# An encoder trunk on one core: the norms' squares summed by TensorE, three chunks at the start of a channel mixer, and the down loads in another order

## The chip, the core and the metric

The kernel runs on one core of a Trainium2 chip. The metric is device time in microseconds. The core has a tensor engine (PE; its weight loads are shown apart as PEld), a vector engine (DVE), a scalar engine (ACT), GpSimd (POOL) and a queue that issues DMAs (SP). Each runs its own list of instructions in order; semaphores tie them together.

## The reference

Two batches (prompt and sample) of 512 tokens with 1024 features pass a trunk of two layers with shared weights, in float32. Layer 0 mixes tokens by windowed means, layer 1 by attention; each is followed by a SwiGLU channel mixer.

```python
def trunk(x, ...):
    for i in range(DEPTH):                       # 2
        h = rms_norm(x, norm_mix[i])
        if i % N_MIXERS == 0: x = x + pool_mixer(h, ...)
        else:                 x = x + attention_mixer(h, ...)
        h = rms_norm(x, norm_ffn[i])
        x = x + swiglu_ffn(h, ...)               # (silu(h Wg) * (h Wu)) Wd, hidden size 2816
def rms_norm(x, g):
    return x * rsqrt(mean(x * x, axis=-1) + EPS) * g
```

## The kernel before

x lies in the on-chip memory with features on the 128 partitions: 8 tiles of features (c) by 2 batches (b) of 512 tokens. Every float32 product is made of three products of split operands: each operand is cast to a rounded high part (ACT) and a low part, the rest (DVE, `..._lo`), and PE multiplies high by high, high by low and low by high.

**Channel mixer.** The two batches and the two halves of each weight matrix form a 2x2 block product, which is computed with seven block products instead of eight (`gate_up(layer, i, k)`, k = 1 to 7). The hidden size is taken in 22 chunks i of 128. One product is 12 matmuls. The moving operands B11, B21 (batch 0), T1, T2, B22, T3, T4 (sums with batch 1) are made once per layer: `b0_full`, `b1_full` scale x by the norm, `t1_full` to `t4_full` subtract (T3 and T4 on POOL, in float32), and `..._hi`, `..._lo` split. The weights of a chunk come as two units (gate and up) into three buffers `raw` (`load_gu`); `block_sums` makes their sums S1 to S4, and `w_split` splits seven tiles into `ring`. `snap_p1`, `snap_p5`, `snap_u2` copy partial sums out of PSUM, `add_c11`, `add_c12`, `add_c22` add to them, `silu_0`, `silu_1`, `hidden_0`, `hidden_1` and `pair_sums` make the hidden values and their sums, which SP stores to device memory (`store_act1`, `store_even`, `store_odd`). Chunks use two sets of three PSUM banks in turn. In the steady state the order of PE is 1, 5, 6, 3, 7, 2, 4. For chunks 0 to 2, where T1 to T4 aren't there yet, the order is written out by hand.

**Down products.** 42 blocks of up to 24 matmuls (`down_block(layer, k)`): for each, ACT and DVE split a piece of weights and a piece of stored hidden values (`block_hi`, `block_lo`). `down_sum(layer, n)` makes weight sums on DVE between the blocks. SP loads hidden pieces (`load_act`, which from the fourth on waits for `block_lo` three blocks before) and weight pieces (`load_wd`; two pieces jj share a semaphore, and a reader waits for both).

**Norm.** For each norm k (1: channel mixer of layer 0; 2: attention; 3: channel mixer of layer 1) ACT squares the tiles of x (`square`), in the order `SEQ[k]`; POOL adds them one by one into `stat[b]` (`add_squares`); PE multiplies that by a matrix of ones, which leaves the sum over all features in every partition (`mean_square`); ACT takes the root of the 128x512 tile (`root`) and DVE its reciprocal (`inverse`). The mixers' work around it is written in order for every engine: in layer 0, PE's `pool(b, c)` (windowed means), `turn_x` (x turned to features on partitions) and `mix(b, g)` (projection), and DVE's `add_mixed`, which adds to x. In attention, `project` makes queries and keys, and `gain`, `head_square` their norm.

## Time and profile before

| | |
|---|---|
| median of 3 runs | 1824.36 us (1822.15 to 1827.1) |
| profiled execution, own time | 1823.22 us |
| its span | 1821.4 us |
| mean granted clock of PE | 0.976 of full |
| PE busy | 1717.3 us (94%), 7741 instructions |
| DVE busy | 1205.1 us (66%) |
| ACT busy | 760.7 us (42%) |
| POOL busy | 202.0 us (11%) |

Times in the rows are microseconds from the span's start. Layer 0's token mixer runs until about 75, its gate/up products until 523, its down blocks until 741, attention until about 1110 to 1144, then layer 1's channel mixer. PEclk and the column of the same meaning in a table of windows give the clock that the chip granted to PE, as a share of 2.4 GHz; 0.5 is 1.2 GHz. In a timeline row the figures are start, time from the first start to the last end, engine, line, operation, operands, count, and in brackets how long the engine had been idle and what it waited for. A busy time of PE overlaps the next instruction's, so lengths are read from start to start.

### The profile page before, as it was taken

The numbers are of one execution on the slowest core, as the hardware profiler recorded it, in microseconds if no ns is written. First come the engines' busy times: TensorE is split into PE (matmuls) and PEld (weight loads), VectorE is DVE, ScalarE is ACT, GpSimd is POOL, SyncE is SP. The second block draws the span as 40 slices with busy tenths as digits, with TensorE's granted clock in tenths as the row PEclk, the third lists the DMA queues.
The fourth block names the chain that finished last, engine by engine and source line by source line (L and its number), as shares of the span: only waits on it lengthen the run. The fifth ranks groups of instructions, "written<-read, shape, count | busy, mean of one in ns | idle before, by whom it ended". The sixth has DMA issues, their size and how long they took to land. (4 is left out here: it accounts for less than half of the span.)

```text
span 1821.4 us, 20998 instructions
## 1 busy us (share of the span) xinstructions
PE 1717.3 (94%) x7741; PEld 1409.0 (77%) x7741; DVE 1205.1 (66%) x1620; ACT 760.7 (42%) x1149; POOL 202.0 (11%) x155
## 2 busy tenths in 40 slices
PE   6779999999999999899998999799999999989998
PEld 6657888888877888778776787578888888878887
DVE  5786656666547756756878877876566665557744
ACT  6543333333333335434576554343333333333332
POOL 1430000000000003322124212500000000000000
PEclk9889999999999999999999999899999999999999
DMA  4003423224275332143112112023233232473333
GB/s 170 24 12 121 129 90 113 93 93 133 76 270 197 101 94 90 58 133 103 42 54 63 35 47 81 24 93 116 87 109 117 93 116 87 156 289 116 95 98 120
DMA packets 185786, 188.40 MB, mean 103 GB/s; under 512 B 8355, under 2 KB 138453, under 8 KB 185685
## 3 DMA queue, kind: packets, MB, share of 16 engines
q1 hardware_dynamic: 112884, 150.36, 25.5%
q10 hardware_dynamic: 72800, 36.70, 6.9%
q8 instruction: 62, 1.02, 0.2%
q14 instruction: 40, 0.32, 0.1%
HBM read 137.23 MB, written 44.56 MB: 100 GB/s over the span
## 5 line engine op out<-in xcount | busy, mean ns | idle before, releaser
L664 PE MATMUL bank<-h_T,ring 128*128 128x512 f32 x2112 | 508.9, 393 | 20.0 <-DVE h_T L1512 11.2
L664 PEld LDWEIGHTS bank<-h_T,ring 128*128 128x128 f32 x2112 | 399.8, 190 | 108.6 <-issue 10.8
L689 PE MATMUL bank<-a,w 128*128 128x512 f32 x1848 | 426.1, 393 | 10.9 <-DVE a L1638 10.9
L689 PEld LDWEIGHTS bank<-a,w 128*128 128x128 f32 x1848 | 349.8, 190 | 85.8 <-issue 12.9
L664 PE MATMUL bank<-h_B,ring 128*128 128x512 f32 x1584 | 388.9, 395 | 9.9 <-ACT tmp L1037 4.3
L664 PEld LDWEIGHTS bank<-h_B,ring 128*128 128x128 f32 x1584 | 300.6, 190 | 78.4 <-ACT tmp L1037 5.2
L1565 DVE TENSOR_TENSOR ring<-raw,ring 128x512 fp32r<-128x512 f32 (+1 forms) x178 | 147.7, 831 | 48.3 <-ACT ring L1016 48.1
L1016 ACT CAST ring<-raw 128x512 fp32r<-128x512 f32 (+1 forms) x178 | 128.5, 722 | 69.7 <-PE bank L664 53.7
L1090 ACT CAST w<-wd_A 128x1024 fp32r<-128x1024 f32 x72 | 70.6, 981 | 199.8 <-PE bank L689 199.8
L1634 DVE TENSOR_TENSOR w<-wd_A,w 128x1024 fp32r<-128x1024 f32 x72 | 82.6, 1147 | 97.3 <-ACT w L1090 97.2
L2112 POOL TENSOR_TENSOR tmp<-tmp,tmp 128x512 f32<-128x512 f32 x42 | 62.5, 1488 | 749.8 <-ACT tmp L938 747.5
L546 PE MATMUL bank<-half_hi,aw 128*128 128x512 f32 x320 | 111.9, 408 | 4.6 <-DVE aw L1459 3.9
L1577 DVE TENSOR_TENSOR tmp<-bank,tmp 128x512 f32<-128x512 f32 x44 | 30.4, 691 | 124.9 <-PE bank L664 124.6
L1638 DVE TENSOR_TENSOR a<-raw,a 128x1024 fp32r<-128x1024 f32 x84 | 97.0, 1154 | 6.5 <-ACT a L1092 6.5
L1092 ACT CAST a<-raw 128x1024 fp32r<-128x1024 f32 x84 | 82.0, 977 | 13.1 <-DMA raw<-act_d 13.1
L546 PE MATMUL bank<-o_hi,aw 128*128 128x512 f32 x256 | 85.6, 397 | 1.5 <-DVE x L1979 1.5
L1016 ACT CAST ring<-s_tmp 128x1024 fp32r<-128x1024 f32 (+1 forms) x46 | 46.7, 1015 | 91.2 <-PE bank L664 85.2
L1343 ACT ACTIVATE prob<-bank,nmax,q_inv 128x512 f32<-128x512 f32 x64 | 49.9, 780 | 70.7 <-DVE nmax L1956 70.7
L546 PEld LDWEIGHTS bank<-half_hi,aw 128*128 128x128 f32 x320 | 61.4, 192 | 19.5 <-issue 3.7
L1053 ACT ACTIVATE tmp<-tmp 128x512 f32<-128x512 f32 x44 | 27.8, 631 | 103.0 <-DVE tmp L1583 103.0
L1565 DVE TENSOR_TENSOR ring<-s_tmp,ring 128x1024 fp32r<-128x1024 f32 (+1 forms) x46 | 54.1, 1177 | 20.7 <-ACT ring L1016 20.7
L1459 DVE TENSOR_TENSOR aw<-raw,aw 128x1024 fp32r<-128x1024 f32 x40 | 54.7, 1369 | 16.6 <-ACT aw L925 16.1
(168 smaller groups left out, 2097.9 us busy)
## 6 DMA issues: line engine op xcount, KB each, us to landing
act_d<-tmp SPq DMA_DIRECT2D x154, 256.0 KB, 3.0
raw<-in_ffn_w_gate_up ACTq DMA_DIRECT2D x70, 512.0 KB, 3.9
raw<-act_d SPq DMA_DIRECT2D x70, 512.0 KB, 3.5
wd_A<-in_ffn_w_down SPq DMA_DIRECT2D x40, 512.0 KB, 6.7
raw<-in_attn_w_qkv SPq DMA_DIRECT2D x24, 512.0 KB, 3.9
raw<-in_ffn_w_gate_up SPq DMA_DIRECT2D x18, 512.0 KB, 4.2
raw<-in_attn_w_o SPq DMA_DIRECT2D x16, 512.0 KB, 4.2
tmp<-tmp SPq DMA_DIRECT2D x80, 64.0 KB, 2.0
```

The lines of the kernel that those rows point to most:

```text
L546: ins = pe.matmul(out, w, m, start=first and i == 0, stop=last and i == n - 1)
L664: ins = pe.matmul(out[:, :], w, m, start=k in (1, 2, 5) and j == 0 and t == 0, stop=k in (2, 3, 4) and j == 3 and t == 2, skip_group_check ...
L689: ins = pe.matmul(banks[m][:, :], w, h, start=q in (0, 1, 3) and first and t == 0, stop=q in (1, 5, 6) and jj == NBLK - 1 and t == 2, skip ...
L1016: nc.scalar.copy(dst, src).then_inc(f_hi, 1)
L1090: nc.scalar.copy(w2[:, k % 3, 0:n, 0, :], src).then_inc(w2_hi, 1)
L1092: nc.scalar.copy(a2[:, (k + 1) % 3, 0:n, 0, :], raw2[:, act_slot(layer, k), 0:n, :]).then_inc(a2_hi, 1)
L1343: nc.scalar.activation(prob[:, i, :], b_score[s % 2][:, :], ACT.Exp, bias=nmax[:, s % 8:s % 8 + 1], scale=q_inv[:, s:s + 1], accum_out=rsu ...
L1459: nc.vector.tensor_tensor(aw[:, slot(i), 1, :], raw[:, i % RAW, :], aw[:, slot(i), 0, :].bitcast(F32), ALU.subtract).then_inc(w_lo, 1)
L1565: nc.vector.tensor_tensor(lo, src, hi.bitcast(F32), ALU.subtract).then_inc(f_lo, 1)
L1634: nc.vector.tensor_tensor(w2[:, k % 3, 0:n, 1, :], src, w2[:, k % 3, 0:n, 0, :].bitcast(F32), ALU.subtract).then_inc(w2_lo, 1)
L1638: nc.vector.tensor_tensor(a2[:, s, 0:n, 1, :], raw2[:, act_slot(layer, k), 0:n, :], a2[:, s, 0:n, 0, :].bitcast(F32), ALU.subtract).then_i ...
L2112: nc.gpsimd.tensor_tensor(out=stat[b][:, :], in0=stat[b][:, :], in1=sqr[i % 2][:, :], op=ALU.add).then_inc(n_acc, 1)
```

## The change

`square` puts some tiles, the set `DIRECT[k]`, into a ring of free tiles. For those PE itself sums over features: `columns` multiplies a square tile (stationary, four times 128x128) by a column of ones and adds into 4 columns of PSUM. For norm 1 all 16 tiles are `DIRECT`, for norm 2 the last four, for norm 3 the last one. What POOL still adds goes through the same `columns`. The result has tokens on partitions, 128x4. ACT takes the root of these 4 columns, DVE their reciprocal and multiplies the unit matrix by it (`diag`), PE multiplies ones by the diagonal (`wide`, 128x512), and ACT copies the result to `stat[b]` (`keep_wide`), or, for `b1_full` of the first four tiles, DVE reads it in PSUM.

A layer's gate/up products begin with chunks 0, 1 and 2, chunk 2 with a third set of banks; its products 1 and 2 move to the start. The tiles of `act_tiles` are laid out anew: three for each chunk; T4 goes to the tile of B11 (after its store), and `silu_0` writes the tile that `silu_1` had. SP stores T1 and B21 ahead of `load_gu(3, 1)`; two A12 pieces are loaded ahead of the last stores, and A21 and A22 come in pairs; `down_sum(n)` follows block n + 4 instead of n + 3. The split of S3 and A12 for chunk 0 comes earlier on ACT and DVE.

The diff, cut to its core:

```diff
+        sq_ring = {1: [tmp[4], tmp[5], tmp[2], tmp[1]], 2: [tmp[4], tmp[5], tmp[0]], 3: [tmp[2]]}
+        diag = {1: tmp[3], 2: tmp[1], 3: tmp[0]}
-        g_bank = [bank[0:3], bank[3:6]]
+        g_bank = [bank[0:3], bank[3:6], [bank[6], bank[7], bank[2]]]
+        DIRECT = {1: SEQ[1], 2: SEQ[2][12:], 3: SEQ[3][15:]}
...
             if i % 2:
-                return act_y
+                return tmp[4], tmp[5], tmp[6]
-            return act_x if j % 2 == 0 else [act_x[3], act_x[1], act_x[2], act_x[0]]
+            return (tmp[0], tmp[1], tmp[2]) if j % 2 == 0 else (tmp[3], tmp[7], tmp[2])
...
+            def columns(src, out, first):
+                for i in range(NT):
+                    ins = pe.matmul(out[:, i:i + 1], src[:, i * P:(i + 1) * P], ones[:, 0:1],
+                                    start=first and i == 0, stop=True, skip_group_check=True)
+            def sum_square(k, r, out):
+                pe.wait_ge(n_sq, 16 * (k - 1) + r + 1)
+                ins = columns(sq_tile(k, r), out, k == 1 and c == 0)
+                ins.then_inc(n_add, 1)
             def mean_square(k, b, out):
-                pe.matmul(out[:, :], ones[:, :], stat[b][:, :], start=True, stop=True).then_inc(n_ms, 1)
+                return columns(stat[b], out, True)
+            def wide(k, b, out):
+                pe.wait_ge(n_diag, 2 * (k - 1) + b + 1)
+                pe.matmul(out[:, :], ones[:, :], diag[k][:, :], start=True, stop=True).then_inc(n_wide, 1)
...
                 for b in range(N_BLOCK):
                     if layer == 0 and b == N_BLOCK - NBLK + 2:
-                        mean_square(2, 0, bank[1])
+                        mean_square(2, 0, bank[1]).then_inc(n_ms, 1)
+                    elif layer == 0 and b == N_BLOCK - NBLK + 4:
+                        wide(2, 0, bank[1])
...
             def inverse(k, b):
                 dve.wait_ge(n_sqrt, 2 * (k - 1) + b + 1)
-                nc.vector.reciprocal(stat[b][:, :], stat[b][:, :]).then_inc(n_rstd, 1)
+                nc.vector.reciprocal(cols, cols).then_inc(n_rstd, 1)
+                nc.vector.tensor_tensor(diag[k][:, :]..., ident[:, :]..., cols..., ALU.mult).then_inc(n_diag, 1)
...
             def silu_0(layer, i):
-                if j > 0 and i % 2 == 0:
-                    act.wait_ge(stored["T3"], 16 * j)
-                elif j > 0:
-                    act.wait_ge(stored["T4"], 16 * j)
+                act.wait_ge(act1, n + 1)
...
-                    if 3 <= k < 27:
-                        down_sum(layer, k - 3)
+                    if 4 <= k < 28:
+                        down_sum(layer, k - 4)
...
-            for r in range(8):
-                add_squares(1, r)
             block_sums_13(0, 0)
             block_sums_24(0, 0)
-            for r in range(8, 16):
-                add_squares(1, r)
```

PE at the start of layer 0's channel mixer, before (L559 is `mean_square`; h_B_80 is B11, h_B_81 is B21, h_T_86 is T1, h_T_82 is T2; a row of L664 or L725 is one product):

```order
L664 MATMUL bank<-h_B_80,ring 128x512 x12
L559 MATMUL bank<-tmp_77,ones 128x512
L664 MATMUL bank<-h_B_81,ring 128x512 x12
L664 MATMUL bank<-h_B_80,ring 128x512 x12
L664 MATMUL bank<-h_T_86,ring 128x512 x12
L664 MATMUL bank<-h_B_81,ring 128x512 x12
L664 MATMUL bank<-h_T_86,ring 128x512 x12
L664 MATMUL bank<-h_T_82,ring 128x512 x12
```

And after, from the same product on (L577 is `columns`, L598 is `wide`):

```order
L725 MATMUL bank<-h_B_80,ring 128x512 x12
L577 MATMUL bank<-ones,tmp_72 128x1 x4
L577 MATMUL bank<-ones,tmp_71 128x1 x4
L725 MATMUL bank<-h_B_81,ring 128x512 x12
L598 MATMUL bank<-tmp_73,ones 128x512
L725 MATMUL bank<-h_B_80,ring 128x512 x12
L725 MATMUL bank<-h_B_81,ring 128x512 x12
L725 MATMUL bank<-h_B_80,ring 128x512 x12
L725 MATMUL bank<-h_T_86,ring 128x512 x12
L725 MATMUL bank<-h_B_81,ring 128x512 x12
L725 MATMUL bank<-h_T_86,ring 128x512 x12
L725 MATMUL bank<-h_T_82,ring 128x512 x12
```

Two products with B operands, (2, 1) and (2, 2), now stand ahead of and between the first ones with T1, and the two last tiles of squares ahead of the second product.

PE at the end of layer 0's down blocks, before (L689 is the down products; 84 are the last four blocks, of 24, 24, 24 and 12):

```order
L664 MATMUL bank<-h_T_84,ring 128x512 x12
L689 MATMUL bank<-a_107,w_106 128x512 x840
L559 MATMUL bank<-tmp_76,ones 128x512
L689 MATMUL bank<-a_107,w_106 128x512 x84
L546 MATMUL bank<-half_hi_50,aw 128x512
```

And after (L750 is the down products):

```order
L725 MATMUL bank<-h_T_84,ring 128x512 x12
L750 MATMUL bank<-a_107,w_106 128x512 x840
L577 MATMUL bank<-ones,tmp_76 128x1 x4
L750 MATMUL bank<-a_107,w_106 128x512 x48
L598 MATMUL bank<-tmp_71,ones 128x512
L750 MATMUL bank<-a_107,w_106 128x512 x36
L564 MATMUL bank<-half_hi_50,aw 128x512
```

The sum is taken at the same place; the product that gives every partition the norm comes two blocks, 48 matmuls, later.

SP behind the last stores of layer 0, before (raw_108 takes the hidden pieces of the down blocks; wd_A_101 is A12, wd_A_102 is A21, wd_A_103 is A22):

```order
L407 DMA raw_108<-act_d 128x1024
L388 DMA wd_A_101<-in_ffn_w_down 128x2x512 x2
L407 DMA raw_108<-act_d 128x1024
L388 DMA wd_A_102<-in_ffn_w_down 128x2x512
L388 DMA wd_A_103<-in_ffn_w_down 128x2x512
L407 DMA raw_108<-act_d 128x512
L388 DMA wd_A_101<-in_ffn_w_down 128x2x512 x2
L407 DMA raw_108<-act_d 128x1024
L388 DMA wd_A_102<-in_ffn_w_down 128x2x512
```

And after:

```order
L424 DMA raw_108<-act_d 128x1024
L405 DMA wd_A_102<-in_ffn_w_down 128x2x512 x2
L424 DMA raw_108<-act_d 128x1024
L405 DMA wd_A_103<-in_ffn_w_down 128x2x512 x2
L424 DMA raw_108<-act_d 128x512
L405 DMA wd_A_101<-in_ffn_w_down 128x2x512 x2
L424 DMA raw_108<-act_d 128x1024
```

The second piece of A21 stood behind the fourth hidden piece of this list and now stands behind the first.

## Rows read from the trace of the kernel before

**Rows 1.** Windows, engine PE: stretch, length, busy (instructions), clock, DMA share, GB/s.
```profile
45.00:140.00 95.00, 73.07 (x295) 0.84 0.08 24
140.00:330.00 190.00, 187.86 (x829) 1.00 0.34 106
```

**Rows 2.** Timeline of PE, start of layer 0's channel mixer.
```profile
41.19 3.22 PE L595 MATMUL bank<-band,xrms 128*128 128x136 f32 x24
47.58 2.07 PE L559 MATMUL bank<-tmp,ones 128*128 128x512 f32 x2 [3.18 <-POOL tmp L2112]
...
56.50 0.47 PE L546 MATMUL bank<-half_hi,pw_hi 128*128 128x512 f32 x1 [0.48 <-ACT x L1111]
...
83.00 2.08 PE L559 MATMUL bank<-tmp,ones 128*128 128x512 f32 x2 [8.53 <-POOL tmp L2112]
...
131.30 5.60 PE L664 MATMUL bank<-h_T,ring 128*128 128x512 f32 x24
136.74 2.88 PE L664 MATMUL bank<-h_B,ring 128*128 128x512 f32 x12
...
149.91 0.50 PE L664 MATMUL bank<-h_B,ring 128*128 128x512 f32 x1 [2.14 <-ACT tmp L1037]
```

**Rows 3.** Timeline of DVE, the same stretch.
```profile
50.41 3.35 DVE L1465 RECIPROCAL tmp<-tmp 128x512 f32<-128x512 f32 x1 [2.59 <-ACT tmp L943]
...
57.33 1.41 DVE L1488 SCALAR_TENSOR_TENSOR f_t<-x,vec,tmp 128x512 f32<-128x512 f32 x2
...
89.66 1.50 DVE L1501 SCALAR_TENSOR_TENSOR f_t<-x,vec,tmp 128x512 f32<-128x512 f32 x1
...
102.32 0.74 DVE L1501 SCALAR_TENSOR_TENSOR f_t<-x,vec,tmp 128x512 f32<-128x512 f32 x1
...
107.83 0.69 DVE L1565 TENSOR_TENSOR ring<-raw,ring 128x512 fp32r<-128x512 f32 x1 [1.09 <-ACT ring L1016]
...
116.39 5.74 DVE L1531 TENSOR_TENSOR h_B<-f_t,h_B 128x512 fp32r<-128x512 f32 x4
```

**Rows 4.** Timeline of ACT: the last moves of x.
```profile
53.10 3.11 ACT L1111 ACTIVATE x<-bank,vec 128x512 f32<-128x512 f32 x5 [0.17 <-PE bank L579]
```

**Rows 5.** Timeline of PE in attention: the sum of one head's squares, and what follows.
```profile
787.33 1.05 PE L781 MATMUL bank<-ones,tmp 128*128 128x1 f32 x8 [1.81 <-ACT tmp L1276]
788.25 0.48 PE L546 MATMUL bank<-half_hi,aw 128*128 128x512 f32 x1
```

**Rows 6.** Timelines of PE and DVE, start of attention.
```profile
721.71 19.65 PE L689 MATMUL bank<-a,w 128*128 128x512 f32 x84
742.97 0.50 PE L546 MATMUL bank<-half_hi,aw 128*128 128x512 f32 x1 [1.61 <-DVE aw L1459]
...
728.79 1.41 DVE L1474 SCALAR_TENSOR_TENSOR tmp<-x,vec,tmp 128x512 f32<-128x512 f32 x2
```

**Rows 7.** Timelines of PE and DVE, start of layer 1's channel mixer.
```profile
1116.79 0.47 PE L546 MATMUL bank<-o_hi,aw 128*128 128x512 f32 x1 [1.54 <-DVE x L1979]
...
1144.08 2.88 PE L664 MATMUL bank<-h_B,ring 128*128 128x512 f32 x12
...
1216.48 4.61 PE L664 MATMUL bank<-h_B,ring 128*128 128x512 f32 x12 [2.20 <-ACT tmp L1037]
...
1156.92 0.80 DVE L1501 SCALAR_TENSOR_TENSOR f_t<-x,vec,tmp 128x512 f32<-128x512 f32 x1
```

**Rows 8.** Timelines of PE and DVE and a window of PE, start of the down blocks.
```profile
549.96 25.40 PE L689 MATMUL bank<-a,w 128*128 128x512 f32 x100 [4.62 <-DVE a L1638]
...
1618.90 31.47 PE L689 MATMUL bank<-a,w 128*128 128x512 f32 x128 [4.82 <-DVE a L1638]
...
546.31 1.23 DVE L1652 TENSOR_TENSOR wd_A<-wd_A,wd_A 128x1024 f32<-128x1024 f32 x1 [10.93 <-DMA wd_A<-in_ffn_w_down]
...
525.00:528.00 3.00, 3.00 (x15) 1.00 0.37 137
```

**Rows 9.** Timelines of DVE and PE, chunk 21 of layer 0: hidden_1, and the last product.
```profile
518.85 0.69 DVE L1589 TENSOR_TENSOR tmp<-tmp,tmp 128x512 f32<-128x512 f32 x1 [0.70 <-ACT tmp L1053]
...
519.98 2.88 PE L664 MATMUL bank<-h_T,ring 128*128 128x512 f32 x12
```

416 lines of the change are left out of this document (264 added, 152 removed).

## The prediction

> **What bounds the kernel now.** I read the table of windows first, then PE's timeline for its idle times, then DVE's and ACT's in the same stretches. The windows [rows 1] show two kinds of stretch: in 140:330 PE is busy 187.86 of 190 us at full granted clock, and there only PE's own work counts; in 45:140 it is busy 73.07 of 95 at a mean clock of 0.84. PE's waits are in few places, and the change touches nearly all of them: the start of each layer's channel mixer (waits of 3.18 and 8.53 us for POOL's sums of squares [rows 2], then a stretch in which DVE has no gap [rows 3]), one wait of 2.14 us [rows 2], the fifth block of the down products, and the start of attention. So the sum is made at five places. Measures used throughout: a gate/up product of 12 matmuls takes 2.72 us at full clock (24 of them from 131.30 to 136.74, [rows 2]), a down block of 24 takes 5.44; a DVE operation on 128x512 takes 0.6 to 0.7 us from start to start.
>
> **Price of the new small sums.** Each square that PE sums is four matmuls of one moving column, eight instructions. The trace has the same pattern for the query heads: it starts at 787.33 and the next matmul at 788.25, so 0.92 us [rows 5]. There are 25 of them: 16 for layer 0's second norm, 4 + 2 in the attention norm, 1 + 2 in the last; 23 us of PE. What they replace are six products of 512 columns, but each norm half now has one such product (the wide one, about 1.0 us at full clock, as before) as well.
> The Trainium skill, TensorE: Matmul & The Clock Gate, section Back-to-back issue gap, gives a floor of about 25 ns from start to start for so few columns; eight would be 0.2 us. Its section on LDWEIGHTS gives 107 ns for each load of 128 columns, 0.86 us for eight. The measured 0.92 us goes with the second; by the first, the 25 sums would cost 5 us instead of 23.
>
> **Down blocks, both layers.** DVE's subtraction for block 4 stands behind down_sum(0), which sat 10.93 us on a weight load (A21's second piece), and PE then waited 4.62 us [rows 8]. The load was issued behind act load 6, which itself waited for block_lo(3). After: both A21 pieces are issued right behind act load 3 and down_sum(0) comes after block_lo(4), so neither is in the way. What could be late next is act load 3, now behind two A12 pieces: block 3 is needed 16.3 us after the first down product, and those pieces go out at 521 to 522, where the DMA engines have room (share 0.37 from 525 to 528, [rows 8]). I take the whole wait as gone. The following 100 matmuls took 25.40 us where 22.9 is full rate, since the granted clock had fallen in the wait: 2.5 more. Layer 1: 4.82 of wait, and 31.47 for 128 instead of 29.2 [rows 8]. Together 14.2 us gained; ends: 7 (half of the waits come back as late transfers) and 14.2.
>
> **Layer 0, start.** PE finishes pool(1, 2) at 44.4 [rows 2]. Four sums end at 48.1, four turns of x (0.12 us per transpose, 1.9) at 50.0, four sums at 53.7, four turns at 55.6, the wide product at 56.5. ACT is behind it: squares 4 to 7 wait for free tiles until 48.7, three casts, then eight moves of 0.61 [rows 4] and a root of 0.3 until 56.7. So mix(1, 0) starts at 57.4 (56.50 before), and b0_full at 58.7 (57.33 before, [rows 3]): nothing is won here, although 3.18 us of wait and the reciprocal of 3.35 us [rows 3] go. From there until gate_up(0, 2) ends PE has four mixes (10.9), four pools (4.1), two products (5.4), eight sums (7.4) and the wide product (0.9), 28.7 us, plus some 1.9 in which it waits for DVE's additions to x: b1_full(0) at 88.0, 89.66 before [rows 3]. The 8.53 us of wait is thus mostly eaten by sums and by the later start. b1_full(4) came 12.7 us later [rows 3] and now has one DVE operation more before it (101.3), then the 1.09 us wait of a ring split on ACT goes [rows 3], since snap_p5 now stands ahead of three casts: B22 is finished at 119.9 rather than 122.1. PE ends product (0, 3) about 1 us later, 2.1 earlier than before; and it has done two products more by then, (2, 1) and (2, 2), worth 5.44. Given back later: with those two no longer as filling, (1, 4) and (2, 4) each wait for add_c22 (0.85 each), (2, 5) waits for S1 of chunk 2, behind c22, hidden_1 and four block sums (1.8), and (2, 7) for snap_u2 behind a split that needs the late unit (3, 1) (0.8): 4.3. The 2.14 us wait of (2, 3) at 149.91 [rows 2] is for tile T1's store, which SP issued behind that same unit and now ahead of it: gained. Sum: 2.1 + 5.4 - 4.3 + 2.1 = 5.4 gained. Bounds: -1 (ACT's order behind the sums costs 4 more, the whole of it DVE's) and 10 (no ping-pong, no gaps).
>
> **Layer 1, start.** Its batch-0 norm: the sum is taken after projection 8 instead of 9, so root and inverse are done when the wide product comes; b0_full starts 2.6 us earlier, and the wait of 1.54 us at 1116.79 goes [rows 7] for 0.9 of extra sum. gate_up(0, 1) then starts at 1143.5 (1144.08, [rows 7]); with it 2.72, two sums 1.84, gate_up(0, 2) 2.72 and the wide product 0.9, b1_full is at 1152.0 rather than 1156.92 [rows 7]: here POOL's last two additions and the reciprocal stood on the path, and little PE work takes their place. From there as in layer 0: 4.9 - 0.6 + 1.1 + 5.4 - 4.3 + 2.2, and 1.7 because the products after 1216.48 ran at half clock (4.61 for 12 instead of 2.88, [rows 7]): 10.4. Bounds 5 and 14.
>
> **Attention, start.** This part costs. The sum of squares is ready before block 38, as before, but the reciprocal now returns as a diagonal, and the wide product that spreads it stands in PE's order before block 40, two blocks of 5.44 later. PE: 721.2 + 0.9 + 10.9 + 0.9 = 733.9, ACT's copy 734.5; norm_full(0, 0) starts at 734.6, not at 728.79 [rows 6]. The whole chain to the first weight split hangs on it, so the first projection comes at 748.8, not 742.97 [rows 6]; PE is through with the down blocks at 742.2 and stands still 6.6 us instead of 1.6, long enough for its clock to fall (it fell in the waits of 4.6). In the first projection PE then has five sums, 4.6 us, in place of a 1.98 us wait and a product. The second half's norm_full starts about 8.5 later. Behind it PE waited 0.56 + 1.65 + 2.27 us for DVE, which takes up what PE is later than DVE; I come out at +6.5. Bounds +2 (all of the later half absorbed) and +10.
>
> **Sum.** -14.2 - 5.4 - 10.4 + 6.5 = -23.5 on the profiled execution's 1823.22 us, which is 1.1 under the median of the runs: 1799.7, taken as **1800**. Its own range, 1792 to 1808.
>
> **Rivals.**
> (1) The small sums and ACT's order eat the starts: layer 0 gives nothing, layer 1 gives 7, attention costs 9. For it: in 57:75 PE was already without a gap, and DVE too [rows 2, 3]. Then 14 + 0 + 7 - 9 = 12: **1811**.
> (2) The down wait is only shifted, since the transfers are near their limit there: half of 14.2 stays, 7: **1807**. Against it: the A12 pieces go out when the queue has room.
> (3) The sums hide and attention's late wide product is absorbed: 14.2 + 10 + 12 - 4 = 32: **1791**. By the page's floor for one column (0.2 us each) this is the case; the row of 0.92 us speaks against it, as does PE's own order of the wide product.
> (4) Slower: silu_0 now writes the tile that hidden_1 reads and so waits for it, in each of 44 chunks. hidden_1 starts at 518.85 and the product that silu_0 waits for anyway ends at 522.9 [rows 9]; the slack is 3.3 us. If something at the steady rate pushes hidden_1 past it, each further microsecond costs 1 us in some 40 chunks, and from 4 us of delay on the kernel is slower: 1800 + 40 = **1840**. Against it: the page has DVE busy for only 66% of the span, and its waits in a chunk are for PE.
> (5) The change does not act: the starts and attention cancel and the down wait is replaced by another: **1822**.
>
> **Chances.** Forecast 0.50, (1) 0.20, (2) 0.08, (3) 0.13, (4) 0.03, (5) 0.06. Faster by over 0.3% (under 1818, about what a measurement of this kernel can tell) is all but (4), (5) and a sliver of (1): 0.89. Same: 0.07. Slower: 0.04. The range 1788 to 1814 takes in (1), (2) and (3) but for their tails.
>
> **What would show it.** In the changed kernel's trace: no PE idle between down blocks 3 and 4; sums of about 0.92 us; b1_full near 88 in layer 0 and 5 us earlier against the layer's start in layer 1; idle of 0.8 to 1.8 us before products (1, 4), (2, 5) and (2, 4), and none before (2, 3); the longest PE wait of the kernel (over 6 us) before the first projection, with half clock behind it. The prediction is wrong if norm_full(0, 0) doesn't come after the wide product by two blocks, if PE waits at block 4 as before, or if steady chunks take more than 19.04 us.

## The result, and the profile after

| | before | changed |
|---|---|---|
| median of the runs | 1823.66 us (6 runs, 1822.15 to 1827.1) | 1815.18 us (6 runs, 1812.64 to 1820.76) |
| profiled execution | 1823.22 us, span 1821.4 | 1813.04 us, span 1811.0 |

The changed kernel takes 0.995 of the time before, 95% interval 0.9932 to 0.9968: faster by 8.5 us, where 24 were forecast. The time lies just outside the predicted range.

The windows answer to [rows 1]. In 45:140 PE is now busy 84.62 us, not 73.07, at a clock of 0.93 and not 0.84, and still layer 0's first down product comes only 1.4 us earlier: the waits were filled with the work of the new norm.

```profile
45.00:140.00 95.00, 84.62 (x426) 0.93 0.07 20
140.00:330.00 190.00, 186.78 (x822) 1.00 0.35 110
```

PE's timeline at layer 0's start in the changed kernel, for [rows 2]. A pair such as (1, 4) is chunk 1, product 4. The first five rows are the first half of the norm, with no gap between them; a wait of 2.52 us for a split comes before (2, 1); then waits where the forecast had them, before (1, 4), (2, 5), (2, 7) and (2, 4), and none before (2, 3).

```profile
43.77 3.63 PE L577 MATMUL bank<-ones,tmp 128*128 128x1 f32 x32
47.26 1.95 PE L619 MATMUL bank<-ident,xin 128*128 128x128 f32 x16
49.04 3.66 PE L577 MATMUL bank<-ones,tmp 128*128 128x1 f32 x32
52.56 3.57 PE L619 MATMUL bank<-ident,xin 128*128 128x128 f32 x16
55.97 1.02 PE L598 MATMUL bank<-tmp,ones 128*128 128x512 f32 x2
...
97.84 3.02 PE L725 MATMUL bank<-h_B,ring 128*128 128x512 f32 x12 [2.52 <-DVE ring L1683]
...
138.96 3.06 PE L725 MATMUL bank<-h_T,ring 128*128 128x512 f32 x12 [0.78 <-DVE tmp L1701]
143.57 5.69 PE L725 MATMUL bank<-h_T,ring 128*128 128x512 f32 x24 [1.56 <-DVE ring L1683]
152.86 3.02 PE L725 MATMUL bank<-h_T,ring 128*128 128x512 f32 x12 [0.88 <-ACT tmp L1141]
156.66 3.04 PE L725 MATMUL bank<-h_T,ring 128*128 128x512 f32 x12 [0.78 <-DVE tmp L1701]
```

Four sums of squares take 3.49 us (43.77 to 47.26), 0.87 each, where [rows 5] gave 0.92. The 16 transposes at 47.26 take 1.78, the same 16 at 52.56 take 3.41: the clock has fallen to half between, though PE never stood still. DVE's timeline of the same stretch, for [rows 3]: `b1_full(0)` at 91.12 behind a wait of 1.72 us for a split, where 88.0 was forecast, and B22's low parts at 117.25, where before they began at 116.39.

```profile
59.21 1.41 DVE L1600 SCALAR_TENSOR_TENSOR f_t<-x,vec,tmp 128x512 f32<-128x512 f32 x2
...
89.67 1.53 DVE L1683 TENSOR_TENSOR ring<-raw,ring 128x512 fp32r<-128x512 f32 x1 [1.72 <-ACT ring L1110]
91.12 0.73 DVE L1618 SCALAR_TENSOR_TENSOR f_t<-x,vec,bank 128x512 f32<-128x512 f32 x1
...
102.67 0.74 DVE L1618 SCALAR_TENSOR_TENSOR f_t<-x,vec,tmp 128x512 f32<-128x512 f32 x1
...
117.25 5.14 DVE L1648 TENSOR_TENSOR h_B<-f_t,h_B 128x512 fp32r<-128x512 f32 x4
```

Attention's start, PE, DVE and a window of PE (length, busy, clock, DMA share, GB/s), for [rows 6]. The diagonal is ready at 714.68; DVE finishes two splits and then has nothing to do for 8.91 us, because the wide product stands in PE's order behind two down blocks. PE pays 6.64 us before the first projection and works at a clock of 0.55 behind it; another 3.85 before projection 2.

```profile
713.99 0.69 DVE L1575 TENSOR_TENSOR tmp<-ident,n_inv 128x512 f32<-128x512 f32 x1
...
725.99 1.42 DVE L1586 SCALAR_TENSOR_TENSOR tmp<-x,vec,tmp 128x512 f32<-128x512 f32 x2 [8.91 <-ACT tmp L1038]
```
```profile
724.31 1.02 PE L598 MATMUL bank<-tmp,ones 128*128 128x512 f32 x2
...
740.17 0.80 PE L564 MATMUL bank<-half_hi,aw 128*128 128x512 f32 x1 [6.64 <-DVE aw L1566]
...
777.87 0.77 PE L564 MATMUL bank<-half_hi,aw 128*128 128x512 f32 x1 [3.85 <-DVE aw L1566]
```
```profile
525.00:528.00 3.00, 3.00 (x15) 1.00 1.05 406
740.00:746.00 6.00, 5.83 (x15) 0.55 0.47 130
```

Down blocks, for [rows 8]: both layers run from their first products without the waits of 4.62 and 4.82 us, though the DMA share in 525:528 is now 1.05 and not 0.37. (Each row ends where the next other instruction or the end of the view stands.)

```profile
521.88 178.44 PE L750 MATMUL bank<-a,w 128*128 128x512 f32 x786 [0.42 <-DVE a L1757]
...
1588.90 185.23 PE L750 MATMUL bank<-a,w 128*128 128x512 f32 x816 [1.17 <-DVE a L1757]
```

Layer 1's start, PE and DVE, for [rows 7]. From its first product (1148.46; its row starts there) to `b1_full` it is now 8.97 us, 12.84 before.

```profile
1148.46 1.75 PE L725 MATMUL bank<-h_B,ring 128*128 128x512 f32 x7
...
1165.25 4.59 PE L725 MATMUL bank<-h_B,ring 128*128 128x512 f32 x12 [2.99 <-DVE ring L1683]
```
```profile
1157.43 0.73 DVE L1618 SCALAR_TENSOR_TENSOR f_t<-x,vec,bank 128x512 f32<-128x512 f32 x1
```

To compare kernels I cut each profile at seven points of PE's timeline: the first gate/up product of layer 0 (GU0), its first down product (DN0), the end of its down products, the start of projection 2 (P2), the first product of layer 1 (GU1), its first down product (DN1), the end of the span. Stretches in us:

| profile of | to GU0 | GU0 to DN0 | down 0 | to P2 | P2 to GU1 | GU1 to DN1 | to end |
|---|---|---|---|---|---|---|---|
| before | 71.6 | 451.7 | 218.1 | 35.5 | 367.2 | 448.0 | 229.4 |
| changed | 81.4 | 440.5 | 211.7 | 44.3 | 370.6 | 440.4 | 222.1 |
| e1_down_only | 69.5 | 453.6 | 210.7 | 35.5 | 371.2 | 448.8 | 222.1 |
| e11_down_t1 | 69.4 | 450.6 | 210.7 | 35.4 | 369.9 | 446.7 | 222.1 |
| e13_last_norm_only | 69.0 | 451.7 | 210.7 | 35.5 | 370.0 | 443.0 | 222.1 |
| e2_wide_early | 88.3 | 442.1 | 211.6 | 36.5 | 370.7 | 442.0 | 222.0 |
| e3_wides_early | 80.3 | 440.4 | 211.6 | 37.2 | 368.4 | 441.6 | 222.0 |
| e4_norm2_old | 86.8 | 439.5 | 210.7 | 35.5 | 367.1 | 443.9 | 223.7 |
| e5_wide_sums | 78.8 | 443.3 | 211.6 | 44.0 | 368.0 | 440.9 | 222.1 |
| e8_two_chunks | 81.5 | 439.5 | 211.6 | 43.3 | 369.2 | 443.4 | 222.1 |
| e6_norm1_pool | 70.5 | 454.2 | 211.6 | 47.8 | 366.9 | 441.3 | 222.1 |
| e12_norm3_old | 81.3 | 439.5 | 211.6 | 46.4 | 370.7 | 448.7 | 223.7 |

Each row is one execution, and the rows come from several chips. The column P2 to GU1, which the change hardly touches, differs by 4 us among kernels alike there: less than that in one profile proves nothing by itself. Part of it is the clock. By the records of the granted clock, the five profiles with less than 16 us at half clock in that stretch have 366.9 to 368.4 us (one of them, e9, is not in the table), the two with 22 us (changed, e2) have 370.6 and 370.7; those with 17 us lie anywhere from 367.2 to 371.2.

### The profile page after: what moved, and what is told of

It reads as the page before. It is cut to its first block, busy times and chain, and to the rows that moved or that the text cites. A ratio compares the mean times of both kernels' runs of the same rounds, so it can differ in the third digit from the quotient of the medians.

```text
span 1811.0 us, 21412 instructions
## 1 busy us (share of the span) xinstructions
PE 1732.8 (96%) x7941; PEld 1428.2 (79%) x7941; DVE 1187.2 (66%) x1628; ACT 761.9 (42%) x1157; POOL 175.2 (10%) x136
## 3 DMA queue, kind: packets, MB, share of 16 engines
q8 instruction: 64, 1.05, 0.2%
## 4 chain that ended last, share of the span: by engine, by line
PE 41%; DVE 4%; issue 2%; ACT 2%; DMA 1%; SPq 0%; POOLq 0%; POOL 0%; DVEq 0%; ACTq 0%
PE bank L725 21%; PE bank L750 12%; PE bank L564 7%; DVE raw_max L2090 1%; ACT pt_hi L1482 1%; PE bank L920 1%; DVE pt_lo L2144 0%; ACT aw L1005 0%; DMA raw<-act_d 0%; DVE nmax L2096 0%; PE bank L772 0%; DVE aw L1566 0%; DVE ring L1683 0%; DVE f_t L1618 0%; DMA raw<-in_ffn_w_gate_up 0%
## 5 line engine op out<-in xcount | busy, mean ns | idle before, releaser
L725 PE MATMUL bank<-h_T,ring 128*128 128x512 f32 x2112 | 502.6, 390 | 16.6 <-DVE ring L1683 6.8
L725 PEld LDWEIGHTS bank<-h_T,ring 128*128 128x128 f32 x2112 | 395.4, 188 | 104.2 <-issue 8.4
L750 PE MATMUL bank<-a,w 128*128 128x512 f32 x1848 | 421.2, 390 | 1.6 <-DVE a L1757 1.6
L750 PEld LDWEIGHTS bank<-a,w 128*128 128x128 f32 x1848 | 346.5, 188 | 74.5 <-issue 2.9
L725 PE MATMUL bank<-h_B,ring 128*128 128x512 f32 x1584 | 388.4, 395 | 7.0 <-DVE ring L1683 5.5
L725 PEld LDWEIGHTS bank<-h_B,ring 128*128 128x128 f32 x1584 | 299.9, 190 | 74.5 <-DVE ring L1683 6.4
L1181 ACT CAST w<-wd_A 128x1024 fp32r<-128x1024 f32 x72 | 70.5, 979 | 177.7 <-PE bank L750 177.7
L564 PE MATMUL bank<-half_hi,aw 128*128 128x512 f32 x320 | 117.7, 427 | 11.8 <-DVE aw L1566 10.5
L1757 DVE TENSOR_TENSOR a<-raw,a 128x1024 fp32r<-128x1024 f32 x84 | 97.2, 1157 | 13.3 <-ACT a L1183 13.3
L2252 POOL TENSOR_TENSOR tmp<-tmp,tmp 128x512 f32<-128x512 f32 x23 | 35.0, 1520 | 656.3 <-ACT tmp L1025 655.6
L1110 ACT CAST ring<-s_tmp 128x1024 fp32r<-128x1024 f32 (+1 forms) x46 | 46.7, 1015 | 82.6 <-PE bank L725 80.3
L564 PE MATMUL bank<-half_lo,aw 128*128 128x512 f32 x160 | 66.3, 414 | 0.0
```

What stands on the lines that cost most here:

```text
L564: ins = pe.matmul(out, w, m, start=first and i == 0, stop=last and i == n - 1)
L725: ins = pe.matmul(out[:, :], w, m, start=k in (1, 2, 5) and j == 0 and t == 0, stop=k in (2, 3, 4) and j == 3 and t == 2, skip_group_check ...
L750: ins = pe.matmul(banks[m][:, :], w, h, start=q in (0, 1, 3) and first and t == 0, stop=q in (1, 5, 6) and jj == NBLK - 1 and t == 2, skip ...
L1110: nc.scalar.copy(dst, src).then_inc(f_hi, 1)
L1181: nc.scalar.copy(w2[:, k % 3, 0:n, 0, :], src).then_inc(w2_hi, 1)
L1757: nc.vector.tensor_tensor(a2[:, s, 0:n, 1, :], raw2[:, act_slot(layer, k), 0:n, :], a2[:, s, 0:n, 0, :].bitcast(F32), ALU.subtract).then_i ...
```

## The experiments

Ratios are to the kernel before, of runs on the same chip; the changed kernel stands at 0.995 (0.9932 to 0.9968). A difference between two ratios whose intervals overlap is called open.

**e1_down_only.** Before, with the changed order of A21, A12 and A22 loads, two A12 pieces ahead, and:

```diff
-                    if 3 <= k < 27:
-                        down_sum(layer, k - 3)
+                    if 4 <= k < 28:
+                        down_sum(layer, k - 4)
```

> The kernel before, with only the third part of the change: the order of the weight loads for the down products, and down_sum one block later. Theory A (the parts add up, and the down part is worth what the forecast said): no wait at down block 4 in either layer, 14.2 us off the kernel before, 1809.5. Theory B (part of that gain in the changed kernel came from its shifted starts): 7 us or less, 1816 or more.

Measured: 1812.6 us, ratio 0.9935 (0.9918 to 0.9952), 11.3 us under before; in the profile 7.4 and 7.3 us in the two down stretches. Theory A for the mechanism and, by the profile, the size; the median lies between the two theories, nearer to A, and the profile lost 4.0 us of the gain between P2 and GU1. This part alone does all that the whole change does: what the rest of it is worth in sum can't be told from nothing.

**e2_wide_early.** The changed kernel with one line:

```diff
-                    elif layer == 0 and b == N_BLOCK - NBLK + 4:
+                    elif layer == 0 and b == N_BLOCK - NBLK + 3:
                         wide(2, 0, bank[1])
```

> The changed kernel with the attention norm's first wide product one block of 24 earlier (before down block 39 and not 40). Theory A (DVE's idle 8.9 us before the first norm_full are PE's own order, and they come out as PE's 6.64 us before the first projection): norm_full starts near 720.6 instead of 725.99, the wait is 1.6, and since the clock no longer falls there another 1 to 2 us come back: 6 to 7 us under the changed kernel, 1808 to 1809. Theory B (the second half of the norm sets the end of this stretch, since its squares come from the last rows of the down products, which do not move): PE's waits move to the projections behind it, and 0 to 2 us are left, 1813 to 1815.

Measured: 1805.92 us, ratio 0.9899 (0.988 to 0.9919). Theory A: PE waits 1.21 us before the first projection, and from the last down product to projection 2 it is 36.5 us and not 44.3. The median is the thing to read here: the profiled execution is the slowest of the six (1815.15 us), and its fall of the clock before GU0 is the longest of all profiles. The same place in the next run's profile, DVE and then PE: norm_full at 719.36, 13.0 us before the end of the down products, where it was 7.6 before it in the changed kernel: earlier by the one block of 5.44 us.

```profile
719.36 1.42 DVE L1586 SCALAR_TENSOR_TENSOR tmp<-x,vec,tmp 128x512 f32<-128x512 f32 x2 [3.49 <-ACT tmp L1038]
```
```profile
717.69 1.02 PE L598 MATMUL bank<-tmp,ones 128*128 128x512 f32 x2
...
733.56 0.50 PE L564 MATMUL bank<-half_hi,aw 128*128 128x512 f32 x1 [1.21 <-DVE aw L1566]
```

**e3_wides_early.** That, and:

```diff
             project(0, b_gate[0], 0, 3)
+            wide(2, 1, b_up[1])
             project(1, b_gate[1], 0, 0)
             project(1, b_gate[1], 0, 1)
-            wide(2, 1, b_up[1])
```

> As the run before, and the second half's wide product right behind projection 0, two quarters of a projection earlier (near 755.6 and not 757.88). Theory A (each wide product's place in PE's order delays DVE): the wait of 3.85 us before projection 2 shrinks by the 2.3 us, 8 to 9 us in all under the changed kernel, 1806 to 1807. Theory B (POOL's split of the second half, 2.5 us for two parts, sets the pace there): no change against the run before.

Measured: 1803.64 us, ratio 0.9888 (0.9868 to 0.9908). PE's wait before projection 2 shrank from 3.85 to 2.95 only, and the stretch did not get shorter (37.2): theory B for the second product, and the difference of the medians to e2_wide_early is open.

**e4_norm2_old.** The changed kernel with the attention norm as before.

```diff
-        DIRECT = {1: SEQ[1], 2: SEQ[2][12:], 3: SEQ[3][15:]}
+        DIRECT = {1: SEQ[1], 2: [], 3: SEQ[3][15:]}
...
-            mean_square(2, 1, b_up[1])
-            for r in range(12, 16):
-                sum_square(2, r, b_up[1])
+            mean_square(2, 1, b_down[3]).then_inc(n_ms, 1)
```

> The changed kernel with the attention norm in the form of before: POOL sums all squares, a sum over 512 columns, root and reciprocal of the whole tile, no wide product, orders of the three engines as before. Theory A (the new form costs 13 us by the attention's leads, 743 to 1022, and not the 6.5 of the forecast): 12 to 13 us under the changed kernel, 1802 to 1803. Theory B (part of the 13 us is the normal loss when PE arrives earlier at a stretch set by DVE and DMA): 6 to 7 us under, 1808 to 1809.

Measured: 1806.01 us, ratio 0.9899 (0.9875 to 0.9924), 9.2 us under the changed kernel by the medians, and 35.5 us to projection 2 instead of 44.3: 8.9. It lies between the two theories, 2.4 above the forecast's 6.5. The stretch behind P2 runs from 366.9 to 371.2 over the table's twelve profiles, with the old norm and the new in no order, so the 3.4 us that the changed kernel's profile lost there are not the norm's.

**e5_wide_sums.** The changed kernel; each square of layer 0's second norm is summed by one product that accumulates over the eight of its half:

```diff
-                ins = columns(sq_tile(k, r), out, k == 1 and c == 0)
-                ins.then_inc(n_add, 1)
+                if k == 1:
+                    pe.matmul(out[:, :], ones[:, :], sq_tile(k, r)[:, :], start=c == 0, stop=c == KC - 1,
+                              skip_group_check=True).then_inc(n_add, 1)
```

> The changed kernel; in layer 0's second norm each square is summed by one product of 512 columns against the tile of ones, eight of them accumulating in one bank, in place of four products of one column; root and reciprocal then go over the whole 128x512 tile, and the two wide products that spread the inverse go. Theory A (the price of the small sums and what they do to the granted clock made layer 0's start no gain): a float32 product of 512 columns takes 0.46 us from start to start (757.88 to 758.33 in the changed kernel's trace), a small sum 0.92, so 16 times 0.46 or 7.4 us of PE less, the clock stays at 1.0 between 44 and 57 us, and after two reciprocals of 3.35 us some 4 to 8 us are left: 1807 to 1811, with the first down product before 519 us. Theory B (DVE sets the pace of that start whatever PE does): the reciprocals stand on the path again and nothing is won, 1814 to 1818.

Measured: 1812.43 us, ratio 0.9929 (0.9913 to 0.9946): open against the changed kernel and between the two theories, with the runs within 5.2 us of each other and the first down product at 522.0, not before 519. One number of the expectation was wrong: four such sums take 3.43 us, 0.86 each, as much as the small ones, not 0.46 (the row that I had taken it from overlaps with its neighbour). So what this run tells is the clock. PE's timeline, then windows with clock in 44:60 for this kernel and for e2_wide_early, which has the small sums:

```profile
43.62 3.60 PE L591 MATMUL bank<-tmp,ones 128*128 128x512 f32 x8
47.05 1.91 PE L626 MATMUL bank<-ident,xin 128*128 128x128 f32 x16
48.80 3.60 PE L591 MATMUL bank<-tmp,ones 128*128 128x512 f32 x8
52.24 1.91 PE L626 MATMUL bank<-ident,xin 128*128 128x128 f32 x16
```
```profile
44.00:60.00 16.00, 15.41 (x81) 1.00 0.01 2
```
```profile
44.00:60.00 16.00, 16.00 (x88) 0.57 0.01 2
```

**e14_first_half_wide.** The same for the first eight squares only, the second eight as changed:

```diff
+                if k == 1 and b == 0:
+                    pe.matmul(out[:, :], ones[:, :], sq_tile(k, r)[:, :], start=c == 0, stop=c == KC - 1,
+                              skip_group_check=True).then_inc(n_add, 1)
+                    return
```

> The changed kernel with the sums of only the first half of layer 0's second norm (the eight between 44 and 57 us) as accumulating products of 512 columns; the second half's eight stay sums of one column. Theory A (the fall of the granted clock in 44 to 60 us follows those eight small sums and the transposes among them): the clock there stays at 1.0 in the profile, the runs keep within 6 us of each other and the kernel comes at 1810 to 1812. Theory B (all sixteen, or PE's busy stretch without a gap, bring it down): the clock falls as in the changed kernel, 1813 to 1816.

Measured: 1814.24 us, ratio 0.9947 (0.9929 to 0.9964); the clock in 44:60 is 1.00 again, the runs lie within 6.5 us. Theory A for the clock and nearly for the spread, theory B for the time.

```profile
44.00:60.00 16.00, 15.41 (x80) 1.00 0.01 2
```

The fall did not go away, it moved: behind the first two of the small sums that are left (at 64.02 us) the clock is at half from 66.4 to 69.8 us. The same 16 windowed-mean matmuls in this profile and in that of e5_wide_sums, which has no fall there, with the same wait of 0.59 us before the sums:

```profile
65.83 3.52 PE L639 MATMUL bank<-band,xrms 128*128 128x136 f32 x16
```
```profile
65.73 2.07 PE L642 MATMUL bank<-band,xrms 128*128 128x136 f32 x16
```

All profiles together: the seven kernels with the small sums there have a clock of 0.57 (once), 0.61 (twice) or 0.89 (four times) in 44:60, and GU0 between 80.3 and 88.3 us; the four with sums over 512 columns have 1.00 in all and GU0 between 78.3 and 81.3. The five where POOL sums have 1.00 three times, 0.79 and 0.89, each with a wait of PE of 3.2 us just before. The runs of one kernel spread by 8 to 14 us in the first group (5 to 12 runs each), 5 to 7 in the second (4 to 6 runs), 2 to 9 in the third (4 to 17 runs): that the small sums make the times spread is likely, not shown.

**e6_norm1_pool.** The changed kernel with layer 0's second norm on POOL, as before:

```diff
-        DIRECT = {1: SEQ[1], 2: SEQ[2][12:], 3: SEQ[3][15:]}
+        DIRECT = {1: [], 2: SEQ[2][12:], 3: SEQ[3][15:]}
...
-            for c in range(4):
-                sum_square(1, c, bank[3])
-            turn_x(1, range(4))
...
+            mean_square(1, 0, bank[3]).then_inc(n_ms, 1)
+            turn_x(1, range(KC))
```

> The changed kernel with layer 0's second norm as before: POOL adds up the squares, one product per half, root and reciprocal of the whole tile; the start with three chunks stays. Theory A (the small sums cost more than POOL's sums made PE wait): the first down product comes at 518 to 520 us in every run, where four profiles of kernels with the small sums had 520.7, 521.9, 526.3 and 530.4, so 3 to 6 us under the changed kernel, 1809 to 1812. Theory B (the forecast: waits of 3.18 and 8.53 us come back and cost what the sums cost): 1815 to 1820.

Measured: 1818.23 us, ratio 0.9958 (0.9943 to 0.9974). DN0 at 524.6, where it is 520.0 in e11_down_t1, which has the same sums and two chunks: PE waits 10.86 us before the sum of the second half and 5.19 before a product of the new order, and over the whole way to DN0 it is idle 4.6 us longer than in e11. Theory B: three chunks begun do not help while the norm comes late.

**e7_split_later.** The changed kernel; in both layers on DVE:

```diff
-                w_split(layer, 1, G_A12)
                 b1_full(layer, 0)
                 t1_full(layer, 0)
+                w_split(layer, 1, G_A12)
```

> The changed kernel, and on DVE in both layers the split of A12 of chunk 1 behind b1_full(0) and its sum, not ahead of them. Theory A (DVE sets PE's pace from b1_full(0) to tile T4, and b1_full(0) waits for this split, 1.72 us of wait and 1.5 of work): b1_full(0) starts at about 89.7 instead of 91.12, and 1 to 2 us are won in each layer, 1811 to 1814. Theory B (the split's wait is only moved: product (1, 2) or DVE waits for it behind b1_full): no change, 1815.

Measured: 1821.67 us (12 runs, 1811.44 to 1824.13), ratio 0.9968 (0.9953 to 0.9984). Theory B: its profile and that of e4_norm2_old have the same clock in 44:60 (0.61), the same GU0 (86.8) and the same stretch to DN0, 439.5, with the split ahead or behind. Its median is above the changed kernel's since nine of the twelve runs lie at 1820 or more and three at 1811 to 1815; the profile is one of the nine, with the long fall of the clock. The mean granted clock of each run goes with this: 0.984 in the three, 0.978 to 0.982 in the nine. That it is the fall in 44:60 which parts the two groups is likely, not shown: no execution of the three has a profile.

**e8_two_chunks.** The changed kernel with the orders of before for the gate/up products on all three engines; on PE:

```diff
                 gate_up(layer, 1, 1)
-                gate_up(layer, 1, 2)
-                gate_up(layer, 2, 1)
                 gate_up(layer, 0, 5)
-                gate_up(layer, 2, 2)
+                gate_up(layer, 1, 2)
                 gate_up(layer, 1, 5)
...
                 gate_up(layer, 1, 7)
+                gate_up(layer, 2, 1)
                 gate_up(layer, 1, 4)
```

> The changed kernel with each layer's gate/up products begun by two chunks in the orders of before on PE, ACT and DVE; norms, tiles, loads and the down part stay as changed. Theory A (the forecast's own balance: 5.4 us from two products done early, 4.3 given back): 1 us per layer slower, 1817. Theory B (layer 1's gain of 6 to 8 us from its first product to its first down product, 440.4 to 443.9 in five profiles against 448.0 and 448.8 in two of the old start, is the three chunks'): layer 1's stretch takes 448 again, and layer 0 loses as much: 1823 to 1829. Theory C (it is the last norm's, whose inverse no longer takes 3.35 us of DVE): layer 1's stretch stays at 441 to 444, 1815.

Measured: 1813.7 us, ratio 0.995 (0.9934 to 0.9966). Theory C, and for layer 0 as well: GU0 to DN0 takes 439.5 us with two chunks, 440.5 with three. In layer 0 the waits of 0.78 to 1.56 us before (1, 4) to (2, 4) are gone again (0.29 is left of them), and nothing is lost for it: up to 125 us PE waits 9.9 us here and 8.3 in the changed kernel, so the two products done early took 1.6 us out of the waits and not 5.44. B22's low parts begin at 115.70, where the changed kernel has 117.25. In layer 1 the stretch is 3.0 us longer, but PE's idle time in it is the same (11.2 and 11.3 us), and PE is at half clock for 17.1 us instead of 6.8. The third chunk is worth nothing that these runs can tell.

```profile
115.70 5.75 DVE L1646 TENSOR_TENSOR h_B<-f_t,h_B 128x512 fp32r<-128x512 f32 x4
```

**e9_sums_wides** has the edits of e5 and e3, shown above, and nothing else; **e10_sums_norm2** those of e5 and e4.

> The changed kernel with the 512-column sums of the run e5_wide_sums and both wide products of the attention norm early, as in e3_wides_early. If the two causes are separate, their gains add: 3.8 us and 11.5 us under the changed kernel, 1799 to 1802, with a spread of the runs near the 5 us of e5_wide_sums and not the 12 of e4_norm2_old. If both had their gain from the same thing (the granted clock over the whole run), the larger stands alone, 1804.

> The changed kernel with the 512-column sums in layer 0's second norm, and the attention norm as before (as in e4_norm2_old). From the first kernel's profile to projection 2 the old norm takes 35.4 us from the last down product, the two early wide products 37.2: 0 to 2 us faster than e9_sums_wides by that, 1798 to 1801; slower than it, 1803, if POOL's four sums of the second half (1.95 us of wait for PE) weigh more.

Measured: 1802.99 us, ratio 0.9885 (0.9872 to 0.9898), and 1803.76 us, 0.9889 (0.9877 to 0.9902), within 5.5 and 4.6 us. Not the sum that was expected: to e3_wides_early (0.9888) the wide sums added nothing that can be measured; its runs spread by 8.5 us, but four or five runs are few to compare spreads by.

**e11_down_t1.** e1 and one line's place on SP:

```diff
                 store_act1(layer, 0)
-                load_gu(sp, layer, 3, 1)
                 store_even(layer, 0)
                 store_act1(layer, 1)
+                load_gu(sp, layer, 3, 1)
                 store_odd(layer, 1)
```

> The kernel of e1_down_only (before with the down part) and one more of the change's edits: on SP the load of unit (3, 1) behind the stores of chunk 0 in both layers. Theory A (the forecast's terms: 2.1 us of wait for tile T1's store in layer 0, 2.2 and 1.7 of clock in layer 1): layer 0's stretch from its first product to the first down product drops from 453.6 to about 451.5, layer 1's from 448.8 to 445, 6 us under e1_down_only, 1806 to 1808. Theory B (the late load then makes chunk 3 wait, or the time was the norm's): 0 to 1 us, 1812.

Measured: 1805.59 us, ratio 0.9887 (0.9873 to 0.9902), against 0.9935 (0.9918 to 0.9952) without it. Theory A: the waits of 2.27 and 2.31 us of e1 before (2, 3) are down to 0.29 each, and the stretches are 3.0 and 2.1 us shorter. Layer 0's product (2, 3), e1 and then e11:

```profile
148.07 4.61 PE L666 MATMUL bank<-h_B,ring 128*128 128x512 f32 x12 [2.27 <-ACT tmp L1039]
```
```profile
146.07 3.01 PE L666 MATMUL bank<-h_B,ring 128*128 128x512 f32 x12 [0.29 <-ACT tmp L1039]
```

**e12_norm3_old.** The changed kernel with the last norm as before:

```diff
-        DIRECT = {1: SEQ[1], 2: SEQ[2][12:], 3: SEQ[3][15:]}
+        DIRECT = {1: SEQ[1], 2: SEQ[2][12:], 3: []}
...
+                if k == 3:
+                    nc.vector.reciprocal(stat[b][:, :], stat[b][:, :]).then_inc(n_rstd, 1)
+                    return
```

> The changed kernel with the last norm in the form of before: POOL's sums, root and reciprocal of the whole tile, no wide product. Theory A (the last norm gives layer 1's gain, since its reciprocal of 3.35 us stands on DVE's path to b1_full): layer 1's stretch from first product to first down product rises from 440 to 444 by 4 to 5 us, and the kernel by as much, 1819 to 1820. Theory B (the gain there is the store's): layer 1's stretch stays, 1815.

Measured: 1827.81 us (12 runs), ratio 1.0013 (0.9999 to 1.0027), as slow as before. Theory A for the place, not for the size: layer 1's stretch is 448.7, 8.3 us longer than in the changed kernel, twice what theory A said. PE is idle 5.0 us longer in it, which is theory A's 4 to 5, and at half clock for 17.1 us instead of 6.8. The medians are 12.6 us apart; where the rest of that lies, the profile does not show in full. POOL adds squares until 1152.7 and forms block sums until 1155.8; DVE's timeline shows the wait for the split of these, then the reciprocal, then two splits, and `b1_full` starts at 1162.50, 13.0 us behind the first product (at 1149.49); PE waits 5.49 us for one of the two splits behind the reciprocal.

```profile
1156.95 1.23 DVE L1698 TENSOR_TENSOR ring<-s_tmp,ring 128x1024 fp32r<-128x1024 f32 x1 [3.68 <-ACT ring L1119]
1158.10 3.34 DVE L1583 RECIPROCAL tmp<-tmp 128x512 f32<-128x512 f32 x1
1161.36 1.22 DVE L1698 TENSOR_TENSOR ring<-raw,ring 128x512 fp32r<-128x512 f32 x2
1162.50 1.77 DVE L1633 SCALAR_TENSOR_TENSOR f_t<-x,vec,tmp 128x512 f32<-128x512 f32 x1
```
```profile
1162.13 7.04 PE L728 MATMUL bank<-h_B,ring 128*128 128x512 f32 x24 [5.49 <-DVE ring L1698]
```

**e13_last_norm_only.** e11 with the new form of the last norm alone, in the orders of two chunks:

```diff
+                else:
+                    mean_square(3, 1, bank[3])
+                    pe.wait_ge(n_sq, 48)
+                    columns(tmp[2], bank[3], False).then_inc(n_ms, 1)
+                    gate_up(layer, 0, 2)
+                    wide(1, bank[5])
```

> The kernel of e11_down_t1 (before with the down part and the store order), and of the change's norms the last one alone: columns for its sums, the small root and inverse, the wide products; two chunks as before. Theory A (the last norm alone is worth what separates the layer 1 stretches of 446.7 without it and 440 to 443.9 with it, and three chunks are worth nothing): layer 1's stretch at 441 to 443, 3 to 6 us under e11_down_t1, which was 20.7 us under the kernel before: 23 to 26 us under before. Theory B (the last norm helps only with three chunks begun, as the 12 us of e12_norm3_old hint, where the wait before the second chunk's product grew to 5.49 us): 0 to 1 us under e11_down_t1.

Measured: 1802.16 us (1798.12 to 1804.13), ratio 0.9872 (0.9853 to 0.9891), 23.4 us under before and the lowest median of all. Layer 1's stretch is 443.0, 3.7 shorter than e11's; its start, counted from attention's last output products, is 0.8 earlier. Theory A by the profile; the difference of the ratios to e11's 0.9887 is open. DVE's timeline, here and then in e11, shows where it comes from: in place of 3.34 us of reciprocal, 0.17 and 0.69, and `b1_full` at 1145.26, 8.3 us behind the first product, where e11 has 12.8 (its row at 1148.83).

```profile
1142.97 0.17 DVE L1514 RECIPROCAL n_inv<-n_inv 128x4 f32<-128x4 f32 x1
1143.17 0.69 DVE L1516 TENSOR_TENSOR tmp<-ident,n_inv 128x512 f32<-128x512 f32 x1
...
1145.26 0.75 DVE L1563 SCALAR_TENSOR_TENSOR f_t<-x,vec,bank 128x512 f32<-128x512 f32 x1 [0.79 <-PE bank L578]
```
```profile
1145.45 3.34 DVE L1467 RECIPROCAL tmp<-tmp 128x512 f32<-128x512 f32 x1
1148.83 1.03 DVE L1503 SCALAR_TENSOR_TENSOR f_t<-x,vec,tmp 128x512 f32<-128x512 f32 x1
```

## Why the prediction was wrong: 24 us forecast, 8.5 measured

The profiled execution came at 1813.04 us where the sum gave 1799.7, 13.3 too low. None of the forecast's own signs of being wrong came: norm_full stands behind the late wide product, PE does not wait at block 4, and the steady chunks kept their pace. It failed in the terms between. By the steps, whose sizes are differences of single profiles and good to about a microsecond at best:

**Small sums: the price right, their effect on the clock missed.** 0.87 us against 0.92. But the sum treated a busy PE as a PE at full clock. In 44:60 PE is busy all 16 us, and the granted clock falls to half for some of them: a mean of 0.89 over 16 us is 3.5 us at half clock in the changed kernel's profile, 0.57 is 13.8 in e2_wide_early's (there the second four sums go from 51.51 to 58.19, 1.67 each). The kernel before is not free of it: its profile has 0.79 there, behind its wait of 3.18 us, where e1, the same up to the down products, has 1.00 and starts its first gate/up product 2.1 us earlier. The Trainium skill, TensorE: Matmul & The Clock Gate, section What's actually happening, has the clock set by how busy PE has been, and its table has the low state after idling. By that rule the stretch would run at full clock in every run; the rows of 0.57 and 0.89 with no gap speak against it, that of e5_wide_sums, 15.41 us busy with 512 columns a sum, goes with it.

**Layer 0's start: 5.4 forecast, 1.4 measured.** This is the first step that failed. Its terms: T1's store 2.1, measured 3.0 (e1 to e11). The norm 2.1, measured -1.0 (DN0 at 520.0 in e11 with POOL's sums, 521.0 in e8 with the new norm, both with two chunks), and that in a run with little fall of the clock: up to DN0 PE is idle 38.3 us in e11 and 24.8 in e8, 13.4 less, and the sixteen small sums, at 0.87 each, are 13.9 us of new work. `b1_full(0)` came at 91.12 and not at 88.0. The third chunk 5.4 - 4.3 = 1.1, measured -0.9 (e8 to changed). The waits that I charged against it came as forecast (0.78, 1.56, 0.88, 0.78: 4.0 for 4.3), but the 5.44 for two products done early never arrived: from `b1_full(0)` to B22's low parts DVE sets the pace, and these begin at 117.25 against 116.39 before, and a product that PE has done ahead of a chain on DVE shortens nothing. With two chunks (e8) they begin at 115.70: the third chunk's DVE work makes that chain longer. My sum added PE's work and DVE's chain instead of taking the longer at each point.

**Layer 1's start: 10.4 forecast, 7.6 in the profile;** the other kernels with the new last norm have 440.9 to 443.9 in the stretch, so 6 is nearer; the changed kernel's profile is at half clock for only 6.8 us there, most of the others for 10 to 17. The last norm's term, 4.9 - 0.6, was right (3.7 + 0.8 from e11 to e13). T1's store gave 2.1 where 2.2 and 1.7 stood: the wait went, the time at half clock did not. The third chunk and the ring split, 5.4 - 4.3 + 1.1, gave nothing that can be told from the clock's part (e8), as in layer 0.

**Attention's start: 6.5 forecast, 8.9 measured,** within its bounds here. Six more kernels with the wide product two blocks late have 7.8 to 12.3; the three of 10.9 and more (e6, e7, e12) are at half clock for 17 to 22 us of the stretch, the others for 10 to 12, the kernel before for 3.4. The mechanism was right step by step: the two blocks' delay, the idle time of 6.6 before the first projection (6.64), the half clock behind it. Too small was what the later half adds: its norm_full was to come 8.5 us later and 2 of them were to be absorbed. Counted from the last down product it came 10.0 later (759.55 less 733.54, before 757.39 less 741.36), and 1.1 were absorbed. How much of this is the clock is not separated. One more step was not taken: the price of this part came from one line's place, and one block earlier it is 1.0 and not 8.9 (e2).

**Behind P2** the profile lost 3.4 us that nothing in the sum answers to. In twelve profiles this column spreads over 4.3 us, and neither form of norm orders it. The changed kernel's profile is at half clock for 22.2 us of it, 8.5 more than the one before, which could cost up to 4.2 us; PE's idle time is the same (26.8 and 26.5). So it is likely the clock of that execution; why the clock fell more often is open.

**Down blocks: right.** -14.2 forecast; 7.4 and 7.3 in e1. In the changed kernel the first contains one wide product more: 6.4 and 7.3.

The misses add up: 4.0 in layer 0, 2.8 in layer 1, 2.4 in attention's start, 3.4 behind P2 and 0.5 in the down blocks are 13.1 of the 13.3. Of the rivals, (1) had the shape: 14 + 0 + 7 - 9 stood there, 13.7 + 1.4 + 7.6 - 8.9 and the 3.4 behind P2 were measured. Of its two reasons the small sums hold (13.9 us of sums for 13.4 of waits in layer 0); nothing in these runs points to ACT's order. Rival (4) never showed: from 160 to 300 us PE is busy 140.00 of 140 us. The chances gave (1) only 0.20, and the range ended between its 1811 and the measured time.

**Where the expected gain went, in one line:** e11, which only reorders loads and puts `down_sum` one block later, is 20.7 us under before; the norms and the third chunk together take 10 to 12 of these back (9.6 between the medians, 11.5 by the ratios), 8.9 of them, by the profile, in attention's norm, 7.8 of which come back when one wide product moves by one block.

## What to carry to other kernels

Measure the parts of a bundle apart: here reordered transfers held the whole gain and the large rewrite gave about half of it back. When work is moved ahead on the busy engine, ask which engine's chain ends last behind it; filling an idle slot there gives nothing if another engine's chain closes the stretch. And where a short step is split over two engines and comes back through a queue in fixed order (here sum, root, diagonal, wide product), look at where each return stands in that order: one line's place was worth 8 to 9 us.

## What the runs showed of the hardware

- A float32 sum of a 128x512 tile as four products of one column takes 0.87 us, as one product of 512 columns against ones 0.86 (3.49 and 3.43 us for four). The price was the same; the granted clock was not, as the next point says.
- PE's granted clock fell to half in 44 to 60 us while PE was busy without a gap, with one-column sums and 128-column transposes, in seven profiles of seven, for 3.5 to 13.8 us by the means; with 512-column sums in the same places in none of four. Where only the first eight sums had 512 columns (e14), it fell at 66.4 us, behind the first two one-column sums.
- The time at half clock in a whole execution runs from 49 to 91 us over the sixteen profiles (90.7 before, 60.9 changed). The mean granted clock differs between runs of one kernel on one chip (0.978 to 0.984 in e7), and in the main the slower runs are the ones with the lower clock.
- After a wait of 6.64 us PE worked at a clock of 0.55 in 740 to 746 us, its first matmul taking 0.80 us; after one of 1.21 at the same place that matmul took 0.50.
- The DMA engines moved 406 GB/s in 525 to 528 us, at a share of 1.05, and no wait of PE followed.
